# Attention put ahead of the recurrence in each pass, with half of a routing inside it

## What is computed

```python
x += W_out(sig(gA) * P_A(SSD(n)) + sig(gB) * P_B(DilatedAttn(n)))
x += PEER(RMSNorm(x))
```

## Time and profile before

| what | value |
|---|---|
| median of 3 runs | 4060.14 us |
| the profiled execution, own time | 4058.57 us |
| its span, first to last instruction | 4056.8 us |
| PE, DVE, ACT, POOL busy | 85%, 71%, 40%, 30% of the span |
| granted TensorE clock, mean | 0.951 |
| DMA | 1444.49 MB, mean 356 GB/s |

### The profile page before, as it was taken

How to read it: one execution, slowest core, us unless ns; L and a number is a source line. 1 busy time by engine, 2 the same in 40 slices (tenths; PEclk the granted TensorE clock), 3 DMA queues, 4 the chain that set the end, 5 groups by cost and what they waited for, 6 DMA issues and landing times.

```text
span 4056.8 us, 40644 instructions
## 1 busy us (share of the span) xinstructions
PE 3436.7 (85%) x13410; PEld 2350.3 (58%) x13410; DVE 2872.2 (71%) x5740; ACT 1612.8 (40%) x4211; POOL 1218.2 (30%) x1094
## 2 busy tenths in 40 slices
PE   7999997989889787888889787988889886777776
PEld 6877875656667564566667564666667562332222
DVE  3632128898887779899787779899788778655444
ACT  4643013566434223676434223576434222222222
POOL 1000002333333224333333224333333224433332
PEclk9999998989999988999999998999999988999999
DMA  6543447999999988999999989999999979999998
GB/s 205 174 160 127 149 138 293 391 364 396 399 421 423 423 315 353 377 398 412 405 425 420 423 311 355 378 395 415 402 425 419 423 278 365 427 427 427 427 427 351
DMA packets 252119, 1444.49 MB, mean 356 GB/s; under 512 B 31608, under 2 KB 31608, under 8 KB 118788
## 3 DMA queue, kind: packets, MB, share of 16 engines
q0 software_dynamic: 164976, 1133.94, 68.6%
q1 hardware_dynamic: 86800, 307.82, 20.4%
q10 hardware_dynamic: 132, 0.12, 0.0%
HBM read 1439.31 MB, written 7.13 MB: 357 GB/s over the span
## 4 chain that ended last, share of the span: by engine, by line
DMA 30%; PE 28%; DVE 24%; ACT 11%; issue 6%; POOL 1%; DVEq 0%; ACTq 0%; POOLq 0%
DMA rows<-in_w_uv,idx 28%; PE banks L592 16%; DVE rows L1451 7%; DVE x L1460 5%; PE sums L851 4%; ACT arena L915 4%; DVE arena L1262 3%; PE banks L851 2%; PE banks L728 1%; ACT L1041 1%; ACT L915 1%; DMA arena<-a_rows 1%; DVE arena L1288 1%; DVE arena L1359 1%; ACT diag L1054 1%
## 5 line engine op out<-in xcount | busy, mean ns | idle before, releaser
L559 POOL DMA_INDIRECT rows<-in_w_uv,idx x1024 | 1170.8, 1143 | 2209.9 <-DVE x L1460 1309.2
L1451 DVE CUSTOM_DVE_ANT_0 rows<-rows,xn 128x1024 f32<-128x1024 f32 x1024 | 1242.3, 1221 | 521.5 <-DMA rows<-in_w_uv,idx 519.3
L592 PE MATMUL banks<-hT,ring 128*128 128x256 f32 x6656 | 1496.2, 382 | 39.7 <-ACT arena L960 17.3
L592 PEld LDWEIGHTS banks<-hT,ring 128*128 128x128 f32 x6656 | 1267.0, 191 | 293.3 <-issue 92.5
L851 PE MATMUL sums<-rows,diag 128*128 128x512 f32 x1648 | 835.3, 644 | 265.8 <-ACT diag L1054 239.7
L851 PEld LDWEIGHTS sums<-rows,diag 128*128 128x128 f32 x1648 | 322.2, 204 | 656.3 <-ACT diag L1054 325.5
L1041 ACT ACTIVATE gelu<-hid 128x2 f32<-128x2 f32 x512 | 103.7, 203 | 1450.9 <-DVE hid L1451 1449.7
L1460 DVE SCALAR_TENSOR_TENSOR x<-rows,wgt,x 128x1024 f32<-128x1024 f32 x484 | 620.3, 1282 | 31.0 <-ACT wgt L1046 30.0
L1262 DVE SCALAR_TENSOR_TENSOR arena<-banks,pr,arena 128x254 f32<-128x254 f32 (+1 forms) x512 | 245.9, 481 | 119.1 <-ACT arena L943 105.3
L851 PE MATMUL banks<-rows,diag 128*128 128x512 f32 x512 | 239.7, 612 | 76.0 <-ACT diag L1054 76.0
L1046 ACT ACTIVATE wgt<-gelu,gate 128x1 f32<-128x1 f32 x1024 | 246.0, 287 | 16.8
(11 more groups left out here) (204 smaller groups left out, 2527.9 us busy)
## 6 DMA issues: line engine op xcount, KB each, us to landing
ring<-in_w_ssd SPq DMA_DIRECT2D x192, 512.0 KB, 7.4
ring<-in_w_att SPq DMA_DIRECT2D x144, 512.0 KB, 7.8
ring<-in_w_mrg SPq DMA_DIRECT2D x128, 512.0 KB, 12.4
arena<-a_rows POOLq DMA_DIRECT2D x32, 1024.0 KB, 11.3
ring<-in_w_qry SPq DMA_DIRECT2D x64, 512.0 KB, 5.0
arena<-bias_tiles POOLq DMA_DIRECT2D x16, 1152.0 KB, 9.7
ring<-in_w_out SPq DMA_DIRECT2D x32, 512.0 KB, 17.9
rows<-in_w_uv,idx POOLq DMA_INDIRECT x1024, 12.5
```

The source lines that it names most:

```text
L559: nc.gpsimd.indirect_dma_start(out=rows[n % NB][:, :], out_offset=None, in_=w_uv, in_offset=bass.IndirectOffsetOnAxis(ap=idx[:, t, s:s + 1 ...
L592: mm = pe.matmul(out, w[:, k * P:(k + 1) * P], rhs[:, k0 + k, :], start=start and k == 0, stop=stop and k == n - 1)
L1451: v.tensor_tensor_reduce(u, u, xn2[:, (n // SLOTS_T) % 3, :], 1.0, 0.0, ALU.mult, ALU.add, hid[:, k:k + 1]).then_inc(u_done, 1)
```

## The change

The phases of a pass become norm, att, ssd, mrg, out and so on, in the plan, in the order of the units and in all five programs. POOL's bias tiles come first in its mixer, tile 0 behind `n_xn(2)` (the two normalised token tiles) and behind `bias_out`, all eight bias DMAs. PE's time-step product moves from behind the norm to behind head pair 3, and waits for `o_ok(4)`, the eviction of bank 4. ACT's and DVE's time-step chain moves to the start of ssd step 0.

What was the last recurrence step's tail in head pair 0 stands in mrg block 0: PE projects units 0, 1 and the half unit 4 (P_B), then does `heads(7)`, then waits for `y_ok(16)`, projects P_A (units 2, 3), and then makes the sum of squares. DVE and ACT make 1/rms there too.

Pieces 0 to 4 of the second tile's routing stand in the four head pairs, pieces 5 to 9 and the gates in ssd steps 0 and 1. For this `ij`, `Ge`, `gsum` and `grec` get room of their own for each tile, and the merge's gate tiles move past the buffers that step 7 still uses. In `BESIDE` the slots of each phase stay as many; the share summed on PE goes from 15% to 30% in att and from 80% to 60% in ssd steps 0 and 1.

```diff
-UNITS = ([("ssd", g, j) for g in range(GROUPS) for j in range(6)] + [("att", i, j) for i in range(4) for j in range(9)]
-         + [("mrg", c, j) for c in range(8) for j in range(5)] + [("out", 0, j) for j in range(8)]
+UNITS = ([("att", i, j) for i in range(4) for j in range(9)] + [("ssd", g, j) for g in range(GROUPS) for j in range(6)]
+         + [("mrg", 0, j) for j in (0, 1, 4, 2, 3)] + [("mrg", c, j) for c in range(1, 8) for j in range(5)]
+         + [("out", 0, j) for j in range(8)]
...
-BESIDE = [("norm", 0, 1, 8, 60), ("ssd", 0, 2, 22, 80), ("ssd", 2, GROUPS, 70, 50), ("att", 0, 4, 65, 15), ("mrg", 0, 8, 42, 5),
+BESIDE = [("norm", 0, 1, 8, 60), ("att", 0, 4, 65, 30), ("ssd", 0, 2, 22, 60), ("ssd", 2, GROUPS, 70, 50), ("mrg", 0, 8, 42, 5),
...
-LATE_PIECES = [(), (0,), (1,), (2,), (), (3,), (4,), (), (5,), (6,), (7,), (), (8,), (9,), (), ()]
-LATE_STEPS = 4
+LATE_HEADS = [(0, 1), (2,), (3,), (4,)]
+LATE_PIECES = [(), (5,), (6,), (7,), (), (8,), (9,), ()]
+LATE_STEPS = 2
...
+                yield place("norm", 0, 0.6)
+                pool.wait_ge(n_xn.sem, n_xn.at(m, 2))
+                pool.wait_ge(bias_out, 16 * 8)
+                bias_tiles(0)
+                for hp in range(1, 4):
+                    yield place("att", hp - 1, 0.75)
+                    pool.wait_ge(s_v.sem, s_v.at(m, hp * 4))
+                    bias_tiles(hp)
                 yield place("ssd", 0, 0.5)
                 pool.wait_ge(dt_T.sem, dt_T.at(m, 2))
...
+                pe.wait_ge(o_ok.sem, o_ok.at(m, 4))
+                pe.wait_ge(par_in, 16 * (m // 2 + 1))
+                for t in range(2):
+                    for k in range(KD):
+                        mm = pe.matmul(pb(4)[:, t * 64:(t + 1) * 64], hT[:, k, t * P:(t + 1) * P],
+                                       pr[:, PW_WDT + 64 * k:PW_WDT + 64 * (k + 1)], start=(k == 0), stop=(k == KD - 1))
+                mm.then_inc(dt_mm.sem, 1)
...
                 for c in range(8):
                     for i in range(2):
                         project(m, "mrg", c, i, free(4 * c + i), hT)
                         yield place("mrg", c, 0.22 * (i + 1))
+                    if c == 0:
+                        project(m, "mrg", c, 4, free(3), oT, n=4)
+                        yield place("mrg", c, 0.55)
+                        heads(GROUPS - 1)
+                        pe.wait_ge(y_ok.sem, y_ok.at(m, 2 * GROUPS))
                     out = free(4 * c + 2)
                     for i in range(2):
                         project(m, "mrg", c, 2 + i, out, yT, start=i == 0, stop=i == 1, k0=8 * i)
                         yield place("mrg", c, 0.22 * (i + 3))
                     if c == 0:
-                        pe.wait_ge(o_ok.sem, o_ok.at(m, 4))
-                    project(m, "mrg", c, 4, free(4 * c + 3), oT, n=4)
+                        pe.wait_ge(z_s.sem, z_s.at(m, GROUPS))
+                        pe.wait_ge(sq_sum.sem, sq_sum.at(m, GROUPS))
+                        for i in range(2):
+                            mm = pe.matmul(pb(5, SEQ), ones, sqsum[:, i, :], start=(i == 0), stop=(i == 1))
+                        mm.then_inc(r_mm.sem, 1)
+                    else:
+                        project(m, "mrg", c, 4, free(4 * c + 3), oT, n=4)
...
-                yield place("att", 0, 0.05)
+                yield place("mrg", 0, 0.0)
                 exps(GROUPS - 1, range(4))
...
+                    if c == 0:
+                        yield place("mrg", 0, 0.72)
+                        after_heads(GROUPS - 1)
+                        yield place("mrg", 0, 1.1)
+                        act.wait_ge(r_ms.sem, r_ms.at(m, 1))
+                        act.activation(rstdB[:, :], rstdB[:, :], ACT.Sqrt).then_inc(r_sq.sem, 1)
...
+                for hp in range(4):
+                    yield place("att", hp, 0.2)
+                    late_routing(hp, 0)
+                    yield place("att", hp, 0.4)
+                    late_routing(hp, 1)
+                    yield place("att", hp, 0.53)
+                    v.wait_ge(bm_in.sem, bm_in.at(m, 16 * hp + 16))
...
-                yield place("att", 0, 0.05)
+                yield place("mrg", 0, 0.02)
                 squares(GROUPS - 2)
-                yield place("att", 0, 0.22)
+                yield place("mrg", 0, 0.4)
                 weigh(GROUPS - 1)
-                yield place("att", 0, 0.33)
+                yield place("mrg", 0, 0.68)
                 after_heads(GROUPS - 1)
-                yield place("att", 0, 0.43)
+                yield place("mrg", 0, 0.85)
                 squares(GROUPS - 1)
...
+                yield place("mrg", 0, 1.05)
+                v.wait_ge(r_mm.sem, r_mm.at(m, 1))
+                v.tensor_scalar(rstdB[:, :], pb(5, SEQ), 1.0 / D_INNER, EPS, ALU.mult, ALU.add).then_inc(r_ms.sem, 1)
+                yield place("mrg", 0, 1.2)
+                v.wait_ge(r_sq.sem, r_sq.at(m, 1))
+                v.reciprocal(rstdB[:, :], rstdB[:, :]).then_inc(r_ok.sem, 1)
```

More of the change, by code:

```diff
@@ L77 @@
 REST = PIECES - PH
-EACH = {"norm": 20.0, "ssd": 42.5, "att": 57.0, "mrg": 20.0, "out": 31.0, "norm2": 14.0, "query": 4.8, "route": 3.0}
-TIMES = {"norm": 1, "ssd": GROUPS, "att": 4, "mrg": 8, "out": 1, "norm2": 1, "query": 2 * PH + 1, "route": REST}
+EACH = {"norm": 20.0, "att": 57.0, "ssd": 42.5, "mrg": 20.0, "out": 31.0, "norm2": 14.0, "query": 4.8, "route": 3.0}
+TIMES = {"norm": 1, "att": 4, "ssd": GROUPS, "mrg": 8, "out": 1, "norm2": 1, "query": 2 * PH + 1, "route": REST}
 AT = {}
@@ L341, in build @@
         zs = [cut(2, SEQ), zs1]
-        spare = used[0]
         used[0] = decays
@@ L612, in mixer @@
                 norm(0)
[L613 to L629, removed]
-                    for d, tri in ((0, le), (1, ge)):
-                        first, second = (0, 1) if d == 0 else (1, 0)
-                        cols = slice(32 * d, 32 * d + 32)
-                        for t, parts in ((first, [(tri, first)]), (second, [(ones, first), (tri, second)])):
-                            for n, (tile, src) in enumerate(parts):
-                                mm = pe.matmul(pb(4)[32 * d:32 * d + 32, 256 + t * P:256 + (t + 1) * P], da[:, src, cols], tile,
-                                               start=(n == 0), stop=(n == len(parts) - 1))
-                    mm.then_inc(dt_cs.sem, 1)
@@ L704, in mixer @@
                         yield place("att", hp, 0.077 * (u + 1))
-                        if hp == 0 and u == 3:
-                            heads(GROUPS - 1)
                     def scores(qt):
@@ new lines, in heads @@
+                def heads(g):
+                    pe.wait_ge(m_ok.sem, m_ok.at(m, 2 * g + 2))
+                    if g:
+                        pe.wait_ge(y_v.sem, y_v.at(m, 2 * g))
+                    else:
+                        pe.wait_ge(dt_T.sem, dt_T.at(m, 2))
+                    for q in range(2):
+                        for si in range(2):
+                            for r in (2 * q, 2 * q + 1):
+                                mm = pe.matmul(pb(4)[64 * (r % 2):64 * (r % 2) + 64, q * SEQ:(q + 1) * SEQ],
+                                               xtok[:, si, r * HD:(r + 1) * HD],
+                                               E[:, r, P + si * SEQ:P + (si + 1) * SEQ], start=(si == 0), stop=(si == 1))
+                    mm.then_inc(y_mm.sem, 1)
@@ L1125, in route @@
                 hs, ks = slice(lo, hi), slice(lo * TOPK, hi * TOPK)
-                cand, half, bits, b16, cvh, ci, over, iint = room[t]
+                cand, half, bits, b16, cvh, ci, over, iint, ij = room[t][0]
+                Ge = room[t][1][0]
                 def link(ins):
@@ L1388, in mixer @@
                     v.wait_ge(m_v.sem, m_v.at(m, 3 * c + 1))
-                    yield place("mrg", c, 0.9)
+                    if c:
+                        yield place("mrg", c, 0.9)
                     v.wait_ge(unit.sem, used_up(m, "mrg", c, 3))
```

296 lines of the change are left out of this document (132 added, 164 removed).

## The result

The changed kernel takes 4087.86 us (median of 4 runs, 4084.17 to 4091.47) where the kernel before takes 4060.05: a ratio of 1.0067, with a 95% interval from 1.0054 to 1.0079. It is slower by some 28 us; 4055 was predicted, with 4029 to 4081 as the range. The profiled execution of after takes 4084.17 us, the lowest of its four, and 25.6 more than that of before.

A forecast was written before the change was run, and what follows sets the result against it. Full DMA engines were taken to bound most of passes 1 to 3, PE's waits pass 0. Pass 0's +13.6 and -18.3 for passes 1 to 3 gave -4.7 on 4058.57, so 4053.9, median 4055, range 4029 to 4081.

The forecast's parts named there:

- (g): Passes 1 to 3, mrg block 0: the recurrence's tail there costs 2.5 us a pass, bounds 0 and 11.
- The tail isn't covered: Passes 1 to 3, mrg block 0: (g) is 11 instead of 2.5, +25.5 for three passes, 4081; chance 0.18.
- (b): Pass 0, head pair 0: PE waits 14 us (12 to 24) on the bias DMAs; +15.6 with the slower clock.
- (a): Pass 0, ahead of the first heads: the wait goes, -11.3 us, and -1.6 for the low clock.
- (c): Pass 0, first mrg block: PE waits for the last recurrence step, +7.3 us; +10.3 with the clock.
- (d): Pass 0, ahead of the time-step product: PE waits for ACT's last eviction, +0.6 us.
- (e): Passes 1 to 3, ssd steps 2 and 3: moving routing pieces gains 7 us a pass, at most 9.4, least nothing.
- (f): Passes 1 to 3, head pair 0: losing the recurrence's tail gives -1.6 us a pass, bounds 0 and -1.6.
- Nothing is gained: Ssd's burst starving POOL moves from step 2 to steps 0 and 1; only pass 0 shows, +13.6, 4074; chance 0.15.
- (h): Passes 1 to 3, attention and ssd steps 0 and 1: the new shares of sums on PE cost 0 us.

The follow-up runs named there:

- e8: e1 with nine slots planned in mrg block 0 in place of some five, and 33 in the seven others; 4073.41 us, ratio 1.003.
- e1: The changed kernel with one slot a pass, the last one due in ssd, summed on DVE instead of PE; 4078.5 us, ratio 1.004.
- e2: The changed kernel with head pair 0's two bias DMAs on their own semaphore and the other six issued after tile 0; 4070.14 us, ratio 1.0016.
- e7: The kernel before, with the last head pair's two bias DMAs issued later, just ahead of the bias tiles; 4045.52 us, ratio 0.9962.
- e4: The changed kernel with all ten pieces of the second tile's routing and the gates back in ssd steps 0 to 3; 4109.02 us, ratio 1.0117.
- e5: The changed kernel with the shares of sums on PE back at 15% in att and 80% in ssd steps 0 and 1; 4082.86 us, ratio 1.0056.
- e10: e7 with the routing's ten pieces spread over ssd steps 0 to 4 instead of 0 to 3; 4036.72 us, ratio 0.9949.
- e3: The changed kernel with the PE-summed slot kept on PE but placed ahead of heads(7) in mrg block 0; 4090.69 us, ratio 1.0063.

## Why the prediction was wrong

**Where it failed: (g), the tail in mrg block 0.** 2.5 us a pass were taken; mrg grew by 9.5, 11.6 and 11.1. The prediction had the place, and as its upper bound 11, "if nothing covers it"; the rival "The tail isn't covered" is what happened, with its condition (a share under 0.8 for 20 us) met by 0.72 over 37.3 us. Two things in the working were wrong. It priced PE's wait, and took the cover from what is in hand: five gathers and six weight units. PE's waits were in fact shorter than thought, 7.3 us against 3.58 + 11. But what sets transfers free is a program order, and the new wait stands in it three times over: ahead of a slot's sum on PE, ahead of P_A's two units, whose ring slots the next weights need, and ahead of the sum of squares, for which DVE holds its own ticks. The gathers stop for 19.28 us, of which PE itself waits 4.17 and 3.16. And out was to catch up: with its share at 1.02 before, it had no transfer time to give.

PE's own delay is a rival: its waits, 4.17 + 3.16, and the slower products behind them, 3.68 for 1.95 and 6.26 for 3.62 (granted clock 0.50 and 0.58), add up to 11.7 us as well. The runs speak against it. In the seven blocks behind PE is busy 114.29 of 123.5 us while the DMA share is 1.02. And in e8 PE waits 15.6 us in pass 2, twice as long, yet mrg takes 152.4 us there and 160.7 in after: more bytes move meanwhile.

Of the 11 us a pass, e1 shows some 3 as the slot on PE. e8 shows that more ticks restore the gathers and cost some of the weights; mrg of its three passes is still 19 us longer than before, of 32. That the rest is the ring held by PE's waits is argued from the DMA queues' rows; a longer ring was not tried.

**(b), the bias wait: right in kind, too small.** 21.18 us in place of 14, and slow products behind it, 1.36 + 0.90 (granted clock 0.50, then 0.86), make 23.4 where 15.6 was taken. PE's arrival at 46.7 came true (40.80 + 5.43), so did the tile's 5.1 (5.4) and the 2.2 behind it (2.1). The eighth issue came at 49.14, not 45.7, and its landing was seen 10.8 us later, not 5.8: the low end was the wrong one. The low end had been taken because PE's wait stops the weight loads. They did stop: from 46.3 to 60 us the DMA view shows no packet of their queue. But POOL had been held for 25.52 us by then, and the eighth DMA, with the DMA engines busy for only 0.16 of that stretch, still took 10.2 us to land. The weight loads were not what made it long. The Trainium skill, "DMA: Bandwidth & Descriptors", section "Anatomy of one DMA — SWDGE (gpsimd) path", had put the bias DMA at an estimated 3.4 us. Here it took those 10.2 us, and with only two of them in the queue (e2) POOL waited 12.65. The measurement decides.

**(a), (c), (d) held.** (a): the wait went (e7 shows it by itself). (c): 4.98 + 3.16 us of wait where 8.3 was left open, and 1.33 + 1.54 of slower products (granted clock 0.59 and 0.82) where 3 was taken; mrg of pass 0 grew by 12.4 for 10.3. (d): 0.48 for 0.6. That the table's first line is only 0.4 off is luck: (b) was 8 us short, and 5.8 us came back that nobody had counted: in the trace of before the clock at the program's start was still low under the time-step product and the units behind it, in that of after it was not (see the last section). Another 2.6 went over to mrg with the tail (head pairs 0 and 1 of pass 0 took 43.9 and 42.5 us, the pairs without it 41.9).

**(e), (f) held in sum, not in place.** -22.6 for -25.8; e4 gives 21 of it to the routing. Steps 2 and 3 came to 40.7 and 39.5 us where 39.9 was said, 9.0 less than before. But step 1 takes 6.0 more than before (44.8 for 38.8), where no change was taken: two thirds of that gain went, as "Nothing is gained" had it, and a gather there comes behind a wait of 9.85 us. Routing and shares have about half of the 6.0 each: step 1 takes 41.9 us with the routing back (e4) and 42.4 with the shares back (e5). The sum comes out because step 0 and head pair 0 together take 4.6 less (45.3 + 59.7 for 53.1 + 56.5), of which (f) had 1.6, and head pairs 1 to 3 2.8 less (161.9 for 164.7).

(h)'s 14 us of routing in attention don't agree with the 10.41 of the earlier trace rows; after has 10.41 there too. Nothing in the sum hangs on it.

**The shape of the miss.** The three losses and the gain were all named. The forecast took the gain (e) at 7 of at most 9.4 and the loss (g) at under a quarter of its bound, in a phase that had been read as full of transfers.

## What to carry to other kernels

In a program whose order is fixed, price a new wait by what is queued behind it on its engine and who is fed by that (here a buffer's release, ring slots, another engine's ticks), not by its own length. A phase that transfers fill completely has nothing to give back, so a stall that holds its transfers up is paid in full. And ask of each gain whether it needs the large change: the wait of (a) came from the place of two DMAs in POOL's queue, moving these alone brings 15 us (e7), and the order of before with that mended (4045.52) is ahead of the reorder with everything mended that was found (4050.29).

## What the runs showed that was not expected

At the start of the program the same products take different times from trace to trace. The time-step product and the three units behind it, timelines of before (its product is in the earlier trace rows), e7 and e10:

```profile
25.05 13.04 PE L592 MATMUL banks<-hT,ring 128*128 128x256 f32 x48
```

```profile
18.02 7.09 PE L623 MATMUL banks<-pr,hT 128*128 128x64 f32 x32 [0.78 <-DVE hT L1222]
24.90 12.37 PE L598 MATMUL banks<-hT,ring 128*128 128x256 f32 x48
```

```profile
17.98 3.79 PE L623 MATMUL banks<-pr,hT 128*128 128x64 f32 x32 [0.78 <-DVE hT L1222]
21.60 10.58 PE L598 MATMUL banks<-hT,ring 128*128 128x256 f32 x48
```

7.09 and 13.04 or 12.37 us, or 3.79 and 10.58. It is the granted clock, though the windows from 18 to 36 us say 1.00 for all three. The clock records of the traces begin only at 30.02 us in before, 28.52 in e7 and 17.51 in e10, and a window counts time without a record as 1.00. Up to the first record the products of the units start 427 ns apart in before and e7, from there on 216 ns, and in e10 216 ns throughout: the two levels of the earlier trace rows, 1.2 and 2.4 GHz. The same window of before and of e10, PE alone, shows it in the count of products:

```profile
25.20:28.20 3.00, 3.00 (x9) 1.00 1.22 299
...
25.20:28.20 3.00, 3.00 (x16) 1.00 1.19 299
```

PE had begun its transposes at 13.7 us in before, 13.6 in e7 and 13.5 in e10. e7 and e10 have the same program up to there; after, e1, e3, e4, e5 and e8 have one program among them, and first records between 16.46 and 22.59 us. So the program up to there doesn't decide it; what does stays open. It is worth some 5 us in pass 0 between e7 and e10. With one trace a kernel, it is not shown whether their other executions differ in the same way.

POOL's eighth DMA from DRAM to DRAM is held, and the profile shows nothing that it waits for: 22.26 us in the earlier trace rows, 25.52 after. Both times it is issued 0.43 us behind the landing of the seventh (at 45.25 and 48.71 us). Where six were issued in a row, behind two and a tile (e2) or ahead of the last two (e7), none was held.
